# First ffn products beside the mixer's last norm, square sums one step later, running sums stored ahead of loads

## The chip, the core and the metric

One core of a Trainium2 chip runs the whole program in one launch. The time is the device time of an execution in microseconds (us); each kernel is run several times and the median counts. Shares and timelines come from one execution that the hardware profiler recorded.

## What is computed

Two transformer blocks over 512 tokens of width 1024, all in float32. The first block scales and shifts its input by a vector `c`, runs a mixer (a state-space scan beside attention), adds and normalizes, and runs an ffn with a squared relu. The second has a windowed attention with a gated unit and 32 routed experts. The change touches the first block alone:

```
h = x * (1.0 + sc1) + sh1
y = hybrid_mixer(h, ...)
x = layer_norm(ALPHA * x + (1.0 + g1) * y, ln1_g, ln1_b)
h = x * (1.0 + sc2) + sh2
ff = square(relu(h @ w_ff_in)) @ w_ff_out
x = layer_norm(ALPHA * x + (1.0 + g2) * ff, ln2_g, ln2_b)

# the end of hybrid_mixer
y_ssm = rms_norm(y * silu(z), ssm_norm_w)
y_att = rms_norm(attention, attn_norm_w)
y = concatenate([y_ssm, y_att]) @ w_out
```

## The kernel before

The program is a row of stages: prepare, streams, mixer, ffn, second, and router with experts. Each stage writes one queue of instructions per engine by hand (TensorE or PE, VectorE or DVE, ScalarE or ACT, GpSimd or POOL, SyncE or SP), and semaphores order them. A stage is a `Block`: at its end all engines meet in a barrier. Behind it stands a second, empty block (`run_stage`, L2867) in which SP clears every semaphore that the stage made, one instruction each, and then all meet again. Only router and experts share one block.

**Weights** go through a ring of four slots (`Weights`, L94). SP loads them in the order of a plan; `upto(sp, stop)` sends the loads up to an entry of the plan, and each load waits until PE has finished with what its slot held. In the plan stand, among others, `z 0`, `z 1` (the streams' last columns), eight `qkv` (one per pair of heads), four `out`, and `up` and `down` of the ffn. A load of 2 MB waits on its own slot alone, but SP's queue is in order, so what stands behind a waiting load waits too.

**Streams** (L348) makes the columns of the scan and of z with 20 groups of matmuls. DVE writes running sums into `sum_rows`; SP stores them to DRAM (L393, L394), behind all its loads of the stage. The mixer reads them back in a broadcast (L923, L928).

**Mixer** (L878): a loop of nine steps. In step j PE projects q, k, v of pair j, scans a chunk and attends for pair j-1; in the ninth step no pair is new, and PE makes the first half products of the out projection instead (`OutProjection`, L681). A tile is 128 tokens; a half product is 8 matmuls of 128x512, one half of the output columns of a tile over the scan's rows (`ssm`) or the attention's (`att`). For the rms norm ACT squares blocks of rows, POOL adds them up (`add_squares`), PE sums over partitions (`square_sums`, L787), and DVE makes the mean (`mean_square`, L823). The bank of these sums is one that a later half product needs, so PE waits for DVE there. In `rest` (L791) PE runs the attention's products for tiles 0 to 3; DVE adds and norms each tile (L839 to L870); PE turns it (`turn_x`, L800), and ACT copies it with scale and shift into `hT` (`columns`, L754; half of the last tile on DVE, L874).

**Ffn** (L1364): each of four groups of 1024 hidden columns has an up and a down product, and each such product is made from seven products of half-size blocks (`SevenProducts`, L1317) in the order P1, P2, P3, P7, P6, P5, P4. P1 and P2 take `hT` of tiles 0 and 1 as it is; the others take sums of `hT`'s quarters that DVE makes (`s_sums`), or weights that DVE has changed in the ring (`t_first`, `t_second`). In an up product one of the seven is 16 matmuls of 128x256 in four blocks (the profile counts each float32 matmul twice, as two passes). P6 goes into P1's banks, so ACT has to copy P1 out first (L1439), and it reads what `t_second` wrote; `t_second` stands on DVE's queue behind the joins that read that copy. At the stage's start POOL clears a tile of zeros, and ACT issues 16 stores of it, 512 KB each, to DRAM (L1435); they stand ahead of the copy of P1 on ACT's queue.

Of the kernel before, what the change touches and what calls it, by code (L numbers as in the profile page):

```python
# [347 lines left out]
def stage_streams(nc, A, G):  # L348

    with ExitStack() as ctx:
# [329 lines left out]
class OutProjection:  # L681
# [84 lines left out]
    def half(self, pe, t, h, k0, bank, depth, done):  # L766
        G = self.G
        for k in depth:
            if t == 0 and h == 0:
                pe.wait_ge(self.w_ok, k0 + k + 1)  # L770
            m = self.nc.tensor.matmul(G.ps[:, bank, :], G.mixT[:, k0 + k, t * P:(t + 1) * P],  # L771
                                      G.W.view(("out", (k0 + k) // 4))[:, k % 4, h * HALF:(h + 1) * HALF],
                                      start=(k == 0), stop=(k == KB - 1))
        if h == 1:
            m.then_inc(done, 1)
# [4 lines left out]
    def att(self, pe, t):  # L780
        for h in range(2):
            self.half(pe, t, h, KB, self.ATT[t][h], range(KB), self.y_done)
# [7 lines left out]

    def rest(self, pe):  # L791

        nc, G = self.nc, self.G

        def turn_x(t):
            pe.wait_ge(self.ln.ready, t + 1)
            if t:
                pe.wait_ge(self.h_ok, KB * t)
            for k in range(KB):
                m = nc.tensor.transpose(G.ps[:, self.TURN[k // 4], (k % 4) * P:(k % 4 + 1) * P], G.X[:, t, k * P:(k + 1) * P],  # L800
                                        G.ident[:])
            m.then_inc(self.turned, 1)
        pe.wait_ge(self.a_done, T)
        nc.tensor.nop().then_inc(G.W.used, 2)
        pe.wait_ge(self.ssm_read, 2)
        self.att(pe, 0)
        pe.wait_ge(self.ssm_read, 3)
        self.att(pe, 1)
        pe.wait_ge(self.ss_read, 2)
        turn_x(0)  # L810
        pe.wait_ge(self.ssm_read, 4)
        self.att(pe, 2)
        turn_x(1)
# [64 lines left out]
def stage_mixer(nc, A, G):  # L878
# [6 lines left out]
    with ExitStack() as ctx:  # L885
# [26 lines left out]
        block = ctx.enter_context(nc.Block())  # L912
# [129 lines left out]
        def _(pe):  # L1042
# [95 lines left out]
            for j in range(PAIRS + 1):  # L1138
# [62 lines left out]
        def _(dve):  # L1201
# [162 lines left out]
def stage_ffn(nc, A, G):  # L1364

    with ExitStack() as ctx:
# [16 lines left out]
        block = ctx.enter_context(nc.Block())  # L1384
# [75 lines left out]
        def _(pe):  # L1460
# [34 lines left out]

            def seven_products(f):
                for name in seven.ORDER:
                    operands_ready(f, name)
                    x, y = x_operand(f, seven.X_OF[name]), y_operand(f, seven.Y_OF[name])
                    for j in range(2):  # L1500
                        bank_ready(f, name, j)
                        out = bank(f, name, j)
                        if f % 2:
                            for k in range(4):
                                m = nc.tensor.matmul(out, x[:, k, j * P:(j + 1) * P], y[:, k, :],  # L1505
                                                     start=(k == 0), stop=(k == 3))
                        else:
                            for b in range(2):
                                at = (2 * j + b) * P
                                for k in range(4):  # L1510
                                    m = nc.tensor.matmul(out[:, b, :], y[:, k, at:at + P], x[:, k, :],  # L1511
                                                         start=(k == 0), stop=(k == 3))
                        m.then_inc(seven.done, 1)
# [12 lines left out]
            def last_down():  # L1526
# [24 lines left out]
        def _(dve):  # L1551
# [81 lines left out]
            def add(n):  # L1633
# [3 lines left out]
                nc.vector.tensor_tensor(y, y, ps[:, 4 + n % 4, :], ALU.add).then_inc(dn_read, 1)  # L1637
            s_sums(0, G.hT)
# [1227 lines left out]

def run_stage(nc, A, G, stage, last=False):  # L2867
# [17 lines left out]
def build(nc, A):  # L2885

    with ExitStack() as ctx:
# [4 lines left out]
        with ExitStack() as first:  # L2892
            G.W = Weights(nc, first, A)
            with ExitStack() as gates:
                G.gate = sbc(gates, "gates", [P, 2, D])
                mixed = ExitStack()
                G.mixT = sbc(mixed, "mixT", [P, 2 * KB, S])
                with ExitStack() as m:
                    G.xbcT = sbc(m, "xbcT", [P, XB, S])
                    G.w_dtf = sbc(m, "w_dtf", [P, KB, 32])  # L2900
                    G.head_rows = sbc(m, "head_rows", [P, 48])
                    G.d_col = sbc(m, "d_col", [P, KB])
                    G.dt = sbc(m, "dt", [P, T, 16])
                    G.av = sbc(m, "rates", [P, T, 32])
                    G.acs = sbc(m, "acs", [P, 64])
                    G.decays = sbc(m, "decays", [P, 128])
                    run_stage(nc, A, G, stage_prepare)
                    run_stage(nc, A, G, stage_streams)
                    G.X = ctx.enter_context(nc.sbuf_tensor("X", [P, T, D], F32, side="right"))
# [58 lines left out]
```

## Time and profile before

| | us |
|---|---|
| median of 3 runs | 2341.12 (2339.7 to 2341.65) |
| the profiled execution, its own time | 2340.7 |
| its span, first to last instruction | 2338.9 |
| streams, from PE's first matmul to the mixer's | 37.6 to 196.5 |
| mixer, to the ffn's first matmul | 196.5 to 600.0 |
| ffn, to the second block's first matmul | 600.0 to 1010.6 |

In a timeline a row is one instruction or several alike in a run: start, length from the first's start to the last's end, engine, line, operation, result and operands, count. In brackets stands how long the engine did nothing before, and who ended it.
### The profile page before, as it was taken

To read this page: it belongs to the slowest core of one execution; us is meant where nothing else is said; L and a number is where in the kernel's file an instruction comes from. 1 tells how busy PE (TensorE), PEld (TensorE's weight loads), DVE (VectorE), ACT (ScalarE), POOL (GpSimd) and SP (SyncE) were. 2 spreads that over 40 slices of the span, in tenths; PEclk is the share of its full clock that TensorE was granted. 3 is DMA by queue.
4 is the path that set the end of the run, shared out by engine and by line. 5 is a ranking of instruction groups with operands and counts; after the bars stand their busy time and mean duration, and the time that the engine had idled before them with its cause. 6 is when DMAs were issued, how large, how long until landed. Compare 5 with 4: busy or idle time off the path is not lost. (4 is left out here: it accounts for less than half of the span.)

```text
span 2338.9 us, 27117 instructions
## 1 busy us (share of the span) xinstructions
PE 2243.1 (96%) x9635; PEld 1068.9 (46%) x9636; DVE 869.9 (37%) x1582; ACT 646.1 (28%) x850; POOL 335.7 (14%) x289
## 2 busy tenths in 40 slices
PE   6998999999799999989898999999999999999997
PEld 2444665644657567535545333333333333333332
DVE  1882666633535365533534122111112111111126
ACT  1211223221010000002300543434343443444430
POOL 4461114440000000001200011010001000010112
PEclk8999999999899999999895999999999999999999
DMA  8463323302623121141007969999999999999997
GB/s 327 189 210 88 82 54 108 135 18 72 234 78 136 75 72 72 55 163 39 1 27 312 377 270 393 421 423 405 424 423 411 422 409 423 422 408 423 422 414 300
DMA packets 139445, 569.43 MB, mean 243 GB/s; under 512 B 12311, under 2 KB 47308, under 8 KB 88172
## 3 DMA queue, kind: packets, MB, share of 16 engines
q1 hardware_dynamic: 123584, 527.89, 57.0%
q0 software_dynamic: 6272, 20.62, 2.2%
q10 hardware_dynamic: 9516, 19.99, 2.2%
q8 instruction: 41, 0.67, 0.1%
q14 instruction: 32, 0.26, 0.0%
HBM read 544.53 MB, written 23.92 MB: 243 GB/s over the span
## 5 line engine op out<-in xcount | busy, mean ns | idle before, releaser
L2656 PE MATMUL banks<-expert_ring,slot_token_gate 128*64 128x512 f32 x2880 | 636.7, 594 | 5.4 <-DMA expert_ring<-in_w_up_dram 3.1
L2656 PEld LDWEIGHTS banks<-expert_ring,slot_token_gate 128*64 128x64 f32 x2880 | 202.3, 137 | 400.2 <-issue 387.0
L2592 ACT COPY expert_ring<-expert_ring 128x2048 f32 x176 | 324.5, 1896 | 75.6 <-DMA expert_ring<-in_w_gate_dram 64.2
L2656 PE MATMUL banks<-expert_ring,slot_xT_gate 128*64 128x512 f32 x1440 | 329.8, 600 | 1.7 <-issue 1.0
L2656 PEld LDWEIGHTS banks<-expert_ring,slot_xT_gate 128*64 128x64 f32 x1440 | 100.6, 138 | 189.3 <-issue 181.9
L2769 DVE TENSOR_SCALAR col_onehot<-banks,slot_gates 128x512 f32<-128x512 f32 x45 | 33.8, 750 | 402.8 <-PE banks L2656 402.7
L521 PE MATMUL banks<-hT,weight_ring 128*128 128x512 f32 x320 | 142.6, 605 | 3.6 <-DMA weight_ring<-in_w_in_dram 2.7
L2754 DVE TENSOR_TENSOR slot_token_gate<-banks,expert_bias_T 128x512 f32<-128x512 f32 x45 | 31.1, 691 | 297.4 <-PE banks L2626 296.4
L2512 POOL COPY slot_ids<-slot_tokens 128x1 int32 (+1 forms) x45 | 8.2, 183 | 891.7 <-PE banks L2626 891.7
L1511 PE MATMUL banks<-hT,weight_ring 128*128 128x256 f32 x512 | 114.5, 384 | 6.6 <-PEq L2878 5.7
L1054 PE MATMUL banks<-hT,weight_ring 128*128 128x512 f32 x256 | 116.1, 604 | 0.0
L771 PE MATMUL banks<-weight_ring,mixT 128*128 128x512 f32 x256 | 112.1, 594 | 3.4 <-DVE rms L823 3.4
L2566 ACT COPY col_onehot<-banks 128x512 f32<-128x512 f32 x45 | 26.4, 586 | 306.8 <-PE banks L2656 306.8
L1511 PEld LDWEIGHTS banks<-hT,weight_ring 128*128 128x128 f32 x512 | 98.2, 192 | 22.9 <-issue 9.4
L521 PEld LDWEIGHTS banks<-hT,weight_ring 128*128 128x128 f32 x320 | 61.2, 193 | 82.4 <-issue 79.5
L1505 PE MATMUL banks<-weight_ring,hidden_T 128*128 128x512 f32 x192 | 84.1, 593 | 0.9 <-PE banks L1511 0.9
L1511 PE MATMUL banks<-token_half_sums,weight_ring 128*128 128x256 f32 x384 | 84.2, 379 | 0.0
L1511 PEld LDWEIGHTS banks<-token_half_sums,weight_ring 128*128 128x128 f32 x384 | 73.0, 190 | 9.9
L771 PEld LDWEIGHTS banks<-weight_ring,mixT 128*128 128x128 f32 x256 | 47.8, 190 | 60.4 <-issue 56.8
L2626 PEld LDWEIGHTS banks<-ident,col_onehot 128*128 128x128 f32 x360 | 37.7, 140 | 75.3 <-issue 66.5
L1054 PEld LDWEIGHTS banks<-hT,weight_ring 128*128 128x128 f32 x256 | 47.6, 193 | 53.0 <-issue 53.0
L2572 ACT COPY col_onehot<-banks 128x512 f32<-128x512 f32 x45 | 26.3, 584 | 165.0 <-PE banks L2656 165.0
(454 smaller groups left out, 2570.3 us busy)
## 6 DMA issues: line engine op xcount, KB each, us to landing
expert_ring<-in_w_gate_dram SPq DMA_DIRECT2D x128, 1024.0 KB, 14.8
expert_ring<-in_w_up_dram SPq DMA_DIRECT2D x128, 1024.0 KB, 13.2
expert_ring<-in_w_down_dram SPq DMA_DIRECT2D x128, 1024.0 KB, 11.8
weight_ring<-in_w_ada_dram SPq DMA_DIRECT2D x12, 2048.0 KB, 11.9
weight_ring<-in_w_in_dram SPq DMA_DIRECT2D x8, 2048.0 KB, 12.1
weight_ring<-in_w_ff_in_dram SPq DMA_DIRECT2D x8, 2048.0 KB, 11.0
weight_ring<-in_w_ff_out_dram SPq DMA_DIRECT2D x8, 2048.0 KB, 10.6
weight_ring<-in_w_in_dram SPq DMA_DIRECT2D x24, 512.0 KB, 5.9
```

The lines of the kernel that those rows point to most:

```text
L521: m = nc.tensor.matmul(ps[:, n % 4, :], w[:, k, b * P:(b + 1) * P], G.hT[:, k, :], start=(k == 0), stop=(k == KB - 1))
L771: m = self.nc.tensor.matmul(G.ps[:, bank, :], G.mixT[:, k0 + k, t * P:(t + 1) * P], G.W.view(("out", (k0 + k) // 4))[:, k % 4, h * HALF:(h ...
L1054: x = nc.tensor.matmul(out, w[:, k, :], G.hT[:, k, :], start=(k == 0), stop=(k == KB - 1))
L1505: m = nc.tensor.matmul(out, x[:, k, j * P:(j + 1) * P], y[:, k, :], start=(k == 0), stop=(k == 3))
L1511: m = nc.tensor.matmul(out[:, b, :], y[:, k, at:at + P], x[:, k, :], start=(k == 0), stop=(k == 3))
L2566: nc.scalar.copy(side_by_side(gate_tok), paired(ps[:, B_G, :])).then_inc(q["g_copied"], 1)
L2572: nc.scalar.copy(side_by_side(up_tok), paired(ps[:, B_U, :])).then_inc(q["u_copied"], 1)
L2592: nc.scalar.copy(flat_ring[:, c * size:(c + 1) * size], flat_ring[:, bass.ds(source + c * size, size)])\
L2626: m = nc.tensor.transpose(ps[:, bank, j * P:(j + 1) * P], cols, G.ident[:])
L2656: x = nc.tensor.matmul(ps[h * CAP:(h + 1) * CAP, bank, :], lhs[:, k % 4, (k // 4) * CAP:(k // 4 + 1) * CAP], X.ring[:, m, k, h * HALF:(h + ...
L2754: nc.vector.tensor_tensor(up, turned_product(B_UT), cols, ALU.add).then_inc(q["u_biased"], 1)
L2769: nc.vector.tensor_scalar(to, ps[:, B_D, :], G.slot_gates[:, at], None, ALU.mult).then_inc(q["y_ok"], 1)
```

## The change

Three edits. The running sums are stored ahead of the load of z 1, and the last of the streams' loads (qkv 3) moves into the mixer's queue. In the mixer's ninth step PE makes the first square sums one step later, and DVE the mean square half a step sooner. And mixer and ffn share one block: the barrier and the clearing between them go, SP's and POOL's ffn parts wait for the last attention product, PE turns tile 2 inside the last attention product, then runs P1 and P2 of the first group with the turn of tile 3 in between.

```diff
--- before.py
+++ after.py
@@ stage_streams, SP @@
-            G.W.upto(sp, G.W.index[("qkv", 0)] + RING)
-
+            G.W.upto(sp, G.W.index[("z", 1)])
             sp.wait_ge(rows_ok, 2)
             sp.dma_start(G.sums_dram[0:16, :], rows[0:16, :]).then_inc(G.sums_out, 16)
             sp.dma_start(G.sums_dram[16:32, :], rows[32:48, :]).then_inc(G.sums_out, 16)
+            G.W.upto(sp, G.W.index[("qkv", 0)] + RING - 1)
@@ OutProjection.rest @@
         pe.wait_ge(self.y_read, 1)
-        self.att(pe, 3)
+        self.att(pe, 3, 0)
+        self.att(pe, 3, 1, range(0, KB // 2))
+        self.turn_x(pe, 2)
+        self.att(pe, 3, 1, range(KB // 2, KB))
         pe.wait_ge(self.y_done, T)
         nc.tensor.nop().then_inc(G.W.used, 2)
-        turn_x(2)
-        turn_x(3)
@@ stage_mixer, PE @@
                     pe.wait_ge(q["proj_read"], 3 * PAIRS)
                     out.ssm(pe, 0, 1)
-                    pe.wait_ge(q["y_read"], PAIRS)
-                    out.square_sums(pe, 0)
                 if old:
...
                 else:
+                    pe.wait_ge(q["y_read"], PAIRS)
+                    out.square_sums(pe, 0)
                     pe.wait_ge(q["state_ready"], PAIRS)
                     out.ssm(pe, 1, 0)
@@ stage_mixer, DVE @@
                 if new:
                     ssm_out(j)
+                else:
+                    out.mean_square(dve, 0)
                 if old:
                     turned(U + 4)
                     softmax(U + 6)
-                    if not new:
-                        out.mean_square(dve, 0)
                     turned(U + 6)
@@ stage_ffn, SP and POOL @@
+            sp.wait_ge(out.y_done, T)
             ln.load(sp)
...
+            pool.wait_ge(out.y_done, T)
             nc.gpsimd.memset(zeros[:], 0.0).then_inc(zeros_ok, 1)
@@ stage_ffn, PE @@
+            def first_products():
+
+                G.W.wait(pe, ("up", 0, 0))
+                pe.wait_ge(out.h_ok, 2 * KB)
+                pe.wait_ge(out.y_read, 3)
+                for j in range(2):
+                    for b in range(2):
+                        up_block(0, "P1", j, b)
+                up_block(0, "P2", 0, 0)
+                out.turn_x(pe, T - 1)
+                up_block(0, "P2", 0, 1)
+                for b in range(2):
+                    up_block(0, "P2", 1, b)
+                pe.wait_ge(out.y_read, T)
+                pe.wait_ge(out.h_ok, T * KB)
+
             def seven_products(f):
-                for name in seven.ORDER:
+                for name in seven.ORDER[2:] if f == 0 else seven.ORDER:
...
+            first_products()
             for f in range(LAST):
                 seven_products(f)
@@ stage_ffn, DVE @@
+            dve.wait_ge(out.h_ok, T * KB)
             s_sums(0, G.hT)
@@ the stages @@
+def stage_mixer_to_ffn(nc, A, G):
+
+    with ExitStack() as ctx:
+        G.block = ctx.enter_context(nc.Block())
+        stage_mixer(nc, A, G)
+        G.mixer_tiles.close()
+        stage_ffn(nc, A, G)
+
...
-                    run_stage(nc, A, G, stage_mixer)
-                mixed.close()
-                run_stage(nc, A, G, stage_ffn)
...
+                run_stage(nc, A, G, stage_mixer_to_ffn)
```

On SP's queue, at the end of streams (`X`, `key_bias`: what the mixer reads of the sums; `weight_ring` 128x8x128: a third of a `qkv` load; `ISA`: the clears). Before:

```order
L141 DMA weight_ring<-in_w_in_dram 128x8x512
L141 DMA weight_ring<-in_w_in_dram 128x8x128 x12
L393 DMA running_sums<-sum_rows 16x512
L394 DMA running_sums<-sum_rows 16x512
L351 UNCONDITIONAL_BRANCH
```

Now:

```order
L392 DMA running_sums<-sum_rows 16x512
L393 DMA running_sums<-sum_rows 16x512
L141 DMA weight_ring<-in_w_in_dram 128x8x512
L141 DMA weight_ring<-in_w_in_dram 128x8x128 x9
L351 UNCONDITIONAL_BRANCH
```

The stores stand ahead of z 1 and three of the four pairs; the fourth pair's three loads went to the next stage.

On PE's queue, in the mixer's ninth step (`ident,probs`: turns of two units; `kT,qT` and `causal_bf`: logits; `mixT`: half products; `ones,xbcT`: the square sums). Before:

```order
L771 MATMUL banks<-weight_ring,mixT 128x512 x8
L787 MATMUL banks<-ones,xbcT 128x1 x4
L1090 MATMUL banks<-ident,probs 128x128 x4
L1076 MATMUL banks<-kT,qT 128x384 x2
L1079 MATMUL banks<-causal_bf,ident_bf 128x128 x2
L771 MATMUL banks<-weight_ring,mixT 128x512 x8
```

Now:

```order
L771 MATMUL banks<-weight_ring,mixT 128x512 x8
L1096 MATMUL banks<-ident,probs 128x128 x4
L1082 MATMUL banks<-kT,qT 128x384 x2
L1085 MATMUL banks<-causal_bf,ident_bf 128x128 x2
L786 MATMUL banks<-ones,xbcT 128x1 x4
L771 MATMUL banks<-weight_ring,mixT 128x512 x8
```

The sums went behind two turns and a step's logits.

On PE's queue, at the mixer's end (`ident,X`: turns of a tile, 8 each; 128x256: blocks of the ffn's products). Before:

```order
L771 MATMUL banks<-weight_ring,mixT 128x512 x16
L800 MATMUL banks<-ident,X 128x128 x16
L885 UNCONDITIONAL_BRANCH
L1459 UNCONDITIONAL_BRANCH
L1511 MATMUL banks<-hT,weight_ring 128x256 x32
L1511 MATMUL banks<-token_half_sums,weight_ring 128x256 x16
```

Now:

```order
L771 MATMUL banks<-weight_ring,mixT 128x512 x12
L797 MATMUL banks<-ident,X 128x128 x8
L771 MATMUL banks<-weight_ring,mixT 128x512 x4
L1468 UNCONDITIONAL_BRANCH
L1509 MATMUL banks<-hT,weight_ring 128x256 x20
L797 MATMUL banks<-ident,X 128x128 x8
L1509 MATMUL banks<-hT,weight_ring 128x256 x12
L1509 MATMUL banks<-token_half_sums,weight_ring 128x256 x16
```

Tile 2 is turned four matmuls ahead of the attention's end, tile 3 behind 20 of the 32 matmuls of P1 and P2, and one branch is left of two with a barrier between. On ACT's queue the order is the same as before: the copies of all four tiles, the 16 stores of zeros, the two copies of P1.

## Rows read from the trace of the kernel before

**Rows 1.** The page: busy time of PE; DMA share in 40 slices
```profile
PE 2243.1 (96%) x9635; PEld 1068.9 (46%) x9636; DVE 869.9 (37%) x1582; ACT 646.1 (28%) x850; POOL 335.7 (14%) x289
...
DMA  8463323302623121141007969999999999999997
```

**Rows 2.** Timeline, streams' end (start us, us, engine, line, op, [idle before <-releaser])
```profile
189.53 0.60 ACT L456 ACTIVATE mixT<-banks 128x512 f32<-128x512 f32 x1 [6.71 <-PE banks L521]
...
193.25 0.42 SPq L394 DMA_DIRECT2D running_sums<-sum_rows  x1
```

**Rows 3.** Timeline of PE, start of the mixer, and a later projection
```profile
196.46 1.09 PE L1109 MATMUL banks<-ident,xbcT 128*128 128x128 f32 x4 [6.96 <-PEq L2878]
...
197.98 15.30 PE L1054 MATMUL banks<-hT,weight_ring 128*128 128x512 f32 x32
...
224.09 7.09 PE L1054 MATMUL banks<-hT,weight_ring 128*128 128x512 f32 x16
```

**Rows 4.** Windows (us, busy of PE, PEld, DVE, ACT, POOL, PEclk, DMA)
```profile
194.00:195.00 1.00, 0.00 (x0) 0.00 (x0) 0.00 (x0) 0.00 (x0) 0.00 (x0) 0.50 1.22 290
...
201.00:202.00 1.00, 1.00 (x4) 0.43 (x3) 0.00 (x0) 0.00 (x0) 0.00 (x0) 1.00 0.64 144
...
488.00:489.00 1.00, 0.00 (x0) 0.00 (x0) 0.80 (x3) 0.98 (x3) 0.00 (x0) 1.00 0.00 0
```

**Rows 5.** Timeline of PE, the mixer's last step
```profile
474.47 1.02 PE L787 MATMUL banks<-ones,xbcT 128*128 128x1 f32 x8 [1.14 <-POOL xbcT L732]
...
489.32 7.13 PE L771 MATMUL banks<-weight_ring,mixT 128*128 128x512 f32 x16 [3.42 <-DVE rms L823]
```

**Rows 6.** Timelines of POOL and DVE, the same step
```profile
468.83 5.49 POOL L732 TENSOR_TENSOR xbcT<-xbcT 128x512 f32<-128x512 f32 x4 [1.26 <-ACT xbcT L741]
...
479.48 0.80 DVE L1223 TENSOR_SCALAR probs<-probs,att_stats 128x384 f32<-128x384 f32 x1
```

**Rows 7.** Timeline of PE, last norm and first ffn products
```profile
585.18 1.06 PE L800 MATMUL banks<-ident,X 128*128 128x128 f32 x8 [0.30 <-PE banks L771]
...
600.03 15.79 PE L1511 MATMUL banks<-hT,weight_ring 128*128 128x256 f32 x64 [5.70 <-PEq L2878]
615.66 7.07 PE L1511 MATMUL banks<-token_half_sums,weight_ring 128*128 128x256 f32 x32
...
629.47 13.98 PE L1511 MATMUL banks<-token_half_sums,weight_ring 128*128 128x256 f32 x64
```

**Rows 8.** Timeline of ACT, the same stretch
```profile
589.36 2.89 ACT L754 ACTIVATE hT<-banks,mod_cols 128x128 f32<-128x128 f32 x8
594.37 1.51 ACT L754 ACTIVATE hT<-banks,mod_cols 128x128 f32<-128x128 f32 x4 [2.12 <-PE banks L800]
600.97 19.42 ACTq L1435 DMA_DIRECT2D expert_rows<-zeros  x16
620.44 1.07 ACT L1439 COPY hidden_T<-banks 128x512 f32<-128x512 f32 x2 [24.56 <-issue]
```

**Rows 9.** Timeline of DVE, the same stretch
```profile
603.69 1.22 DVE L1344 TENSOR_TENSOR hT<-hT 128x1024 f32<-128x1024 f32 x1
...
623.59 2.28 DVE L1359 TENSOR_TENSOR weight_ring<-weight_ring 128x2048 f32<-128x2048 f32 x1
```

**Rows 10.** The line that issues the zero stores (duration ns, first and last start)
```profile
L1435 ACTq DMA_DIRECT2D expert_rows<-zeros x16: 396/1272/1902, 601.0 to 619.1; - x16
```

**Rows 11.** Timeline, ffn to the second block, and that to the router
```profile
1007.98 0.69 DVE L1671 COPY hT<-banks 128x512 f32<-128x512 f32 x1 [1.91 <-PE banks L1522]
...
1010.55 0.34 SPq L1725 DMA_DIRECT2D sink_row<-in_sinks_dram  x1
...
1235.22 0.13 DVE L2120 TENSOR_SCALAR neg_top<-top 128x1 f32<-128x1 f32 x1
...
1239.00 0.38 ACTq L2214 DMA_DIRECT2D hT<-in_b_gate_dram  x1
```

**Rows 12.** Timeline of PE, router to experts inside one merged block
```profile
1263.89 3.95 PE L2402 MATMUL banks<-place_onehot,hT 32*128 32x32 f32 x32
```

More of the change, by code:

```diff
@@ L773, in half @@
                                       start=(k == 0), stop=(k == KB - 1))
-        if h == 1:
+        if h == 1 and KB - 1 in depth:
             m.then_inc(done, 1)
@@ L778, in ssm, with att @@
         self.half(pe, t, h, 0, self.SSM[t][h], depth, self.a_done)
-    def att(self, pe, t):
-        for h in range(2):
-            self.half(pe, t, h, KB, self.ATT[t][h], range(KB), self.y_done)
+    def att(self, pe, t, h, depth=range(KB)):
+        self.half(pe, t, h, KB, self.ATT[t][h], depth, self.y_done)
     def square_sums(self, pe, m):
@@ L789, in square_sums, with turn_x @@
         x.then_inc(self.ss_done, 1)
+    def turn_x(self, pe, t):
+        G = self.G
+        pe.wait_ge(self.ln.ready, t + 1)
+        if t:
+            pe.wait_ge(self.h_ok, KB * t)
+        for k in range(KB):
+            m = self.nc.tensor.transpose(G.ps[:, self.TURN[k // 4], (k % 4) * P:(k % 4 + 1) * P], G.X[:, t, k * P:(k + 1) * P],
+                                         G.ident[:])
+        m.then_inc(self.turned, 1)
     def rest(self, pe):
         nc, G = self.nc, self.G
[L795 to L802, printed above, removed]
         pe.wait_ge(self.a_done, T)
@@ L911, in stage_mixer @@
         out = OutProjection(nc, ctx, A, G)
-        block = ctx.enter_context(nc.Block())
+        G.out = out
+        block = G.block
         @block.sync
@@ L1383, in stage_ffn @@
         ln = Norm(nc, ctx, G, "ln2", A["ln2_g"][0:1, :], A["ln2_b"][0:1, :])
-        block = ctx.enter_context(nc.Block())
+        out = G.out
+        block = G.block
         def x_quarter(src):
@@ L1494, in bank_ready, with up_block @@
                     pe.wait_ge(seven.joined, 16 * g + 3 + j)
+            def up_block(f, name, j, b):
+                x, y = x_operand(f, seven.X_OF[name]), y_operand(f, seven.Y_OF[name])
+                at = (2 * j + b) * P
+                for k in range(4):
+                    m = nc.tensor.matmul(bank(f, name, j)[:, b, :], y[:, k, at:at + P], x[:, k, :],
+                                         start=(k == 0), stop=(k == 3))
+                if b:
+                    m.then_inc(seven.done, 1)
@@ new lines, in down_block @@
+            def down_block(f, name, j):
+                x, y = x_operand(f, seven.X_OF[name]), y_operand(f, seven.Y_OF[name])
+                for k in range(4):
+                    m = nc.tensor.matmul(bank(f, name, j), x[:, k, j * P:(j + 1) * P], y[:, k, :],
+                                         start=(k == 0), stop=(k == 3))
+                m.then_inc(seven.done, 1)
+            def first_products():
[12 more added lines that the diff above has]
+                pe.wait_ge(out.h_ok, T * KB)
@@ L1496, in seven_products @@
             def seven_products(f):
-                for name in seven.ORDER:
+                for name in seven.ORDER[2:] if f == 0 else seven.ORDER:
                     operands_ready(f, name)
-                    x, y = x_operand(f, seven.X_OF[name]), y_operand(f, seven.Y_OF[name])
                     for j in range(2):
                         bank_ready(f, name, j)
-                        out = bank(f, name, j)
                         if f % 2:
-                            for k in range(4):
-                                m = nc.tensor.matmul(out, x[:, k, j * P:(j + 1) * P], y[:, k, :],
-                                                     start=(k == 0), stop=(k == 3))
+                            down_block(f, name, j)
@@ L1507, in seven_products @@
                         else:
                             for b in range(2):
[L1509 to L1513, printed above, removed]
+                                up_block(f, name, j, b)
                 pe.wait_ge(seven.done, 14 * (f + 1))
@@ L2895, in build @@
                 G.gate = sbc(gates, "gates", [P, 2, D])
[L2896 to L2909, printed above, removed]
-                    run_stage(nc, A, G, stage_mixer)
-                mixed.close()
-                run_stage(nc, A, G, stage_ffn)
+                G.mixer_tiles = m = ExitStack()
+                G.mixT = sbc(m, "mixT", [P, 2 * KB, S])
+                G.xbcT = sbc(m, "xbcT", [P, XB, S])
+                G.w_dtf = sbc(m, "w_dtf", [P, KB, 32])
+                G.head_rows = sbc(m, "head_rows", [P, 48])
+                G.d_col = sbc(m, "d_col", [P, KB])
+                G.dt = sbc(m, "dt", [P, T, 16])
+                G.av = sbc(m, "rates", [P, T, 32])
+                G.acs = sbc(m, "acs", [P, 64])
+                G.decays = sbc(m, "decays", [P, 128])
+                run_stage(nc, A, G, stage_prepare)
+                run_stage(nc, A, G, stage_streams)
+                G.X = ctx.enter_context(nc.sbuf_tensor("X", [P, T, D], F32, side="right"))
+                run_stage(nc, A, G, stage_mixer_to_ffn)
             G.w_router = ctx.enter_context(nc.sbuf_tensor("w_router", [P, KB, EXPERTS], F32, side="right"))
```

13 lines of the change are left out of this document (8 added, 5 removed).

## The prediction, made before the changed kernel was run

> **What bounds the kernel now.** I read the page first. TensorE is busy for 96% of the span, and the DMA slices are mostly under half up to slice 21 and full from slice 25 on [rows 1]: up to the router the kernel is bound by PE's chain with its gaps, in the experts by the stream of weights. The stages run one behind the other, so what a gap loses ahead of the router comes off the end, unless something behind was waiting for other reasons; the diff touches nothing there. So the question is which of PE's gaps close. I went along PE's timeline and looked at each idle time of over 1 us, then at the engine named as its releaser.
>
> Three places matter. At the streams' end PE stands still for 6.96 us [rows 3]. ACT's last work ends at 190.13, but SP issues its second store of the running sums as late as 193.25 to 193.67 [rows 2]: SP holds the barrier. The granted clock falls to 0.50 (1.2 GHz) in this gap and is back at 1.00 (2.4 GHz) by 201 [rows 4]. In the mixer's last step PE waits 1.14 us for POOL's sum of squares and 3.42 us for DVE's mean square [rows 5]. At the mixer's end PE turns tile 2 at 585.18, then tile 3 waits, then comes the barrier; the ffn starts at 600.03 [rows 7], at half clock.
>
> **The change part by part.** I keep the times of before as the ruler, each part against its own place.
>
> *Sums stored ahead of loads (A).* The two stores move ahead of the z 1 load, far ahead of PE's end; the three loads of pair 3, which wait for z 1's products, move into the mixer behind its first two small loads. They aren't needed before pair 3. SP has nothing left to do at the end, so the last is ACT at 190.13 [rows 2]. What the barrier takes is bounded by the others: 196.46 less 193.67 = 2.8 us here with 28 semaphores to clear, and 1010.55 less 1008.67 = 1.9 us with 24 [rows 11]. I take 2.5: PE starts at 192.6, 3.9 us sooner. Its gap is then 3.1 us, and over a gap of 3.42 us the clock stayed at 1.00 [rows 4, 5]. So the slow start should go too: 1.1 us by 15.30 against twice 7.09 [rows 3], at most 2.3 (half of 196.46 to 201). I take 1.8, which the same slow start costs in the ffn (15.63 us from start to start for 64 matmuls against 13.81) [rows 7]. A gives 5.7 us.
>
> *Square sums a step later (B).* PE, free at 473.33 (474.47 less the wait), now turns two units and makes the next logits first, ten instructions; I estimate 1.5 us for them, and POOL is done at 474.32 [rows 6]. DVE takes the mean square behind the softmax that ends at 480.28 [rows 6] and no longer behind the next one; PE asks for it at 489.32 - 4.6 = 484.7. DVE doesn't wait for it, as the sums are made by 476. Both waits go: 1.14 + 3.42 = 4.6 us. Nothing else is late: the softmax that now follows has the 7.13 us of the next half product to hide in [rows 5].
>
> *The ffn in the mixer's block (C).* Tile 2 is turned inside the last attention product, which ends 0.9 us later (eight transposes, 1.06 us [rows 7]), at 585.8; with 0.3 us of wait P1 starts at 586.1. It needs tiles 0 and 1 alone. P1 and one of P2's four blocks are 40 of 64 matmuls of 0.216 us [rows 7], 8.6 us: 594.7. Tile 3 is normed by then (ACT's copy of tile 2 ends at 592.25 + 0.9 [rows 8]) and is turned without a wait, until 595.6. Copies of it take 1.5 us [rows 8], the four sums on DVE 4.9 us (600.03 to 604.91 [rows 9]): the third product can start at 602.1, while PE ends P2 at 600.8. 1.3 us lost. Third and fourth take 13.8 us [rows 7]: PE is at the fifth (P6) at 615.9, 13.6 us sooner than 629.47.
>
> But P6 needs the bank of P1 and weights that DVE makes after it read P1's copy, and ACT copies P1 only behind its 16 stores of zeros. These took 600.97 to 620.39, then the copies from 620.44 [rows 8], and DVE's weights were ready at 625.87 [rows 9], 5.4 us behind the copies' start. Before, that was 3.6 us ahead of PE, so it cost nothing; now that cover is gone. In the new order the stores still stand behind ACT's last copies, which end at 597.2. With the same 19.5 us the P1 copies start at 616.7, the weights are there at 622.1, and P6 starts at 622.2: 7.2 us sooner, with a gap of 6.3 us ahead of it. Over such a gap the clock fell [rows 3, 4], so the slow start of 1.8 us that the ffn's beginning had is only moved to P6. The loss of the old start lies within 629.47; the new one comes behind 622.2. So C gives 7.2 - 1.8 = 5.4 us.
>
> Is 19.5 us right? The 16 issues have a median of 1272 ns, a shortest of 396 and a longest of 1902 [rows 10]; 512 KB each in 1272 ns is 412 GB/s, so I hold the train for bound by the transfer and not by ACT. The 4 MB of down weights are asked for at 585.8, as before at 585.0, and by the rate of the train take some 10 us: they are through when the stores begin. Only the two rows of gain and shift stand beside the stores, as before. The Trainium skill (DMA: Bandwidth & Descriptors, "Issuing engines are not separate DMA queues") says that SP's and ACT's transfers share the same 16 DMA engines and interleave; by it, loads still under way would stretch the train, and the sum would turn into the third rival's, while the rows give the one above.
>
> The branch at the seam costs nothing visible: router and experts lie in one block like this, and PE's 32 matmuls across that seam take 3.95 us without a gap [rows 12].
>
> *The longer clear (D).* The mixer's 54 semaphores are no longer cleared at 596 to 600 but with the ffn's 24 at the next barrier. Barriers took 1.88 us with 24, 3.65 with 55 [rows 11], 4.15 with 54 (595.88 to 600.03 [rows 7, 8]): 0.057 to 0.076 us each, so 3.1 to 4.1 us more. I take 3.4. It falls on the chain; nothing covers it.
>
> Sum: 5.7 + 4.6 + 5.4 - 3.4 = 12.3 us. The profiled execution's own time is 2340.7 us (span 2338.9), 0.4 us under the median of the three: **2328.4 us**.
>
> **The rivals.** *The train does not bind.* If ACT's issues go at the shortest one's 396 ns [rows 10], they end at 603.5, the weights are ready by 612, and P6 starts at 615.9 with no gap before it. C gives 13.6: 20.5 us in all, 2320.2 us. Against it: the median.
>
> *The streams' end isn't SP's.* If the barrier waits for something else, or for the stores' landing as well, A gives nothing: 2334.1 us. For it: a barrier of 2.8 us with 28 semaphores is longer than the 0.06 us each would make it (2.1); against it: SP is the only engine with work after 190.13.
>
> *The train is slowed by the loads it now meets.* Place: ACT's queue from 597. If ACT's stores get half of the DMA engines all along, an issue takes 2.43 us, the train ends at 636.1, P6 starts at 641.6, 12.1 us later than before. 5.7 + 4.6 - 12.1 - 1.8 - 3.4 = -7.0: 2347.7 us, slower. It decides from a train of 31.8 us on, 1.99 us an issue; the longest single issue was 1902 ns [rows 10]. It needs 8 MB of loads beside the stores, and some 1 MB is left by then.
>
> **How the numbers follow.** Forecast 0.74, streams 0.13, train that doesn't bind 0.06, slow train 0.03; 0.04 is left for a new wait of a few us in the mixer's first step, whose small loads I only moved. The bounds of the unknown costs: A 4.6 to 6.6, train 1.5 us either way, D 3.1 to 4.1: 2325 to 2332 for the forecast alone. Taking in the streams' rival gives **2323.5 to 2334.5**. A measurement of this kernel can tell 0.2%, 4.7 us. Faster by more than that are the forecast, the first two rivals and part of the rest: 0.91. Slower 0.03, the same 0.06.
>
> **What would show it.** In the new profile: PE's gap ahead of the mixer is near 3 us and the clock stays at 1.00; no wait of PE for POOL's squares or DVE's mean square; PE's matmuls of P1 run on from the attention's; a gap of 1 to 2 us ahead of the third product; a gap of about 6 us ahead of P6, released by DVE, with ACT's stores of zeros ending just under 6 us before its end; a barrier of about 5.3 us between ffn and second block. I am wrong if P6 has no gap, if the gap is over 10 us, if the first gap stays near 7, or if the experts' stage changes its length by more than 2 us.

## The result, and the profile after

The kernel after takes 2320.67 us in the median of five (2314.18 to 2323.31), the kernel before beside it 2339.7 (2335.32 to 2341.65): a ratio of 0.9913, interval 0.9892 to 0.9934. That is 19.0 us less where 12.3 were forecast, below the range's lower end of 2323.5. The profiled execution of after took 2315.37 us (span 2313.2), 25.7 us less of span than that of before.

Where it came from, in the two profiled executions (shift: how much sooner the same instruction starts than in before):

| place | before | after | shift | gained here | on record |
|---|---|---|---|---|---|
| ACT's last work in streams | 189.53 | 188.33 | 1.2 | 1.2 | not part of the change (below) |
| first half product of the mixer | 213.20 | 208.33 | 4.87 | A 3.7 | 5.7 |
| half product behind the mean square | 489.32 | 479.54 | 9.78 | B 4.9 | 4.6 |
| P6, the ffn's fifth product | 629.47 | 606.47 | 23.0 | C 13.2 | 5.4 |
| second block's first projection | 1010.60 | 991.17 | 19.4 | D -3.6 | -3.4 |
| router's first count | 1241.08 | 1215.40 | 25.7 | 6.3 | 0 |

The streams' last matmul ends at 186.5 to 189.5 us in the thirteen profiles of this document, whichever order the stores have (189.50 in before, 186.58 in e7, which has the same streams), so the 1.2 us are one execution's and not the change's.

The timelines of ACT and PE at the mixer's start answer to [rows 2, 3], the windows to [rows 4]:

```profile
188.33 0.60 ACT L456 ACTIVATE mixT<-banks 128x512 f32<-128x512 f32 x1 [6.71 <-PE banks L521]
```

```profile
191.51 0.63 PE L1115 MATMUL banks<-ident,xbcT 128*128 128x128 f32 x4 [3.22 <-PEq L2922]
...
192.30 15.60 PE L1060 MATMUL banks<-hT,weight_ring 128*128 128x512 f32 x32
208.33 1.09 PE L1135 MATMUL banks<-X 128*64 128x128 f32 x16 [0.43 <-DVE X L1260]
```

```profile
193.00:194.00 1.00, 1.00 (x2) 0.44 (x2) 0.00 (x0) 1.00 (x1) 0.00 (x0) 0.50 0.57 158
...
197.00:198.00 1.00, 1.00 (x4) 0.51 (x3) 0.53 (x1) 0.53 (x1) 0.00 (x0) 1.00 0.97 243
```

The barrier runs from ACT's end at 188.93 to 191.51, 2.6 us, and PE's gap is 3.2 instead of 7.0 us. But the clock falls to 0.50 behind this gap too, so the 32 projections keep a slow start (15.60 us, 15.30 before), and there is a new wait of 0.43.

In the mixer's last step both waits of [rows 5] are gone:

```profile
469.80 1.00 PE L786 MATMUL banks<-ones,xbcT 128*128 128x1 f32 x8
...
479.54 7.09 PE L771 MATMUL banks<-weight_ring,mixT 128*128 128x512 f32 x16
```

At the seam, PE's timeline against [rows 7]:

```profile
571.46 1.04 PE L797 MATMUL banks<-ident,X 128*128 128x128 f32 x8
...
576.23 8.87 PE L1509 MATMUL banks<-hT,weight_ring 128*128 128x256 f32 x40 [0.30 <-PE banks L771]
584.94 1.04 PE L797 MATMUL banks<-ident,X 128*128 128x128 f32 x8
585.81 5.35 PE L1509 MATMUL banks<-hT,weight_ring 128*128 128x256 f32 x24
592.58 7.14 PE L1509 MATMUL banks<-token_half_sums,weight_ring 128*128 128x256 f32 x32 [1.42 <-DVE hT L1350]
599.56 7.07 PE L1509 MATMUL banks<-hT,weight_ring 128*128 128x256 f32 x32
606.47 13.98 PE L1509 MATMUL banks<-token_half_sums,weight_ring 128*128 128x256 f32 x64
```

Up to the third product all is as forecast: the 40 matmuls take 8.87 us (8.6 on record), the wait ahead of the third is 1.42 (1.3). The gap of 6.3 us ahead of P6 isn't there. ACT's timeline, and ACT's issues of zeros with their landing (shortest, median, longest), show why, against [rows 8, 10]:

```profile
586.01 0.46 ACT L754 ACTIVATE hT<-banks,mod_cols 128x128 f32<-128x128 f32 x1 [2.72 <-PE banks L797]
586.02 0.40 ACTq L1444 DMA_DIRECT2D expert_rows<-zeros  x1
...
587.45 11.20 ACTq L1444 DMA_DIRECT2D expert_rows<-zeros  x13
598.69 1.07 ACT L1448 COPY hidden_T<-banks 128x512 f32<-128x512 f32 x2 [11.17 <-issue]
```

```profile
L1444 ACTq DMA_DIRECT2D expert_rows<-zeros x16: 396/549/1330, 586.0 to 597.3; - x16
...
DMA to landing us min/median/max: 7.0/12.9/15.1
```

The 16 issues take 12.6 us instead of 19.4, a median of 549 ns instead of 1272, and a store lands 12.9 us behind its issue (median) instead of 7.4. What stands beside the stores has changed, too: SP asked for the two rows of gain and shift at 600.0, just ahead of the stores, and asks for them at 577.0 now, right behind the down weights. SP's timeline of before, then of after:

```profile
600.00 0.34 SPq L647 DMA_DIRECT2D ln_gb<-in_ln_g_dram  x1
600.39 0.45 SPq L648 DMA_DIRECT2D ln_gb<-in_ln_b_dram  x1
```

```profile
576.05 0.92 SPq L141 DMA_DIRECT2D weight_ring<-in_w_ff_out_dram  x2
577.01 0.50 SPq L647 DMA_DIRECT2D ln_gb<-in_ln_g_dram  x1
577.56 0.65 SPq L648 DMA_DIRECT2D ln_gb<-in_ln_b_dram  x1
```

ACT copies P1 at 598.69, DVE's weights are made 601.84 to 604.12, and PE comes to P6 at 606.47 without a gap. At the ffn's end the barrier takes from 985.81, the end of DVE's last copy, to 991.17, 5.4 us for 78 clears [rows 11]:

```profile
991.17 9.31 PE L1851 MATMUL banks<-hT,weight_ring 128*64 128x512 f32 x34 [6.08 <-PEq L2922]
```

The last 6.3 us lie in the second block, which the diff doesn't touch. PE waits 2.37 us there for POOL's probabilities in both kernels; what differs is the clock behind the wait. Timeline and windows of before, then of after:

```profile
1121.88 1.53 PE L1871 MATMUL banks<-ident,probs 128*128 128x128 f32 x8 [2.37 <-POOL probs L1753]
1123.34 3.78 PE L1858 MATMUL banks<-k2T,q2T 64*128 64x256 f32 x8
```

```profile
1125.00:1130.00 5.00, 5.00 (x22) 3.24 (x22) 4.06 (x13) 0.87 (x2) 0.00 (x0) 0.50 0.00 0
```

```profile
1101.30 1.09 PE L1906 MATMUL banks<-ident,probs 128*128 128x128 f32 x8 [2.37 <-POOL probs L1788]
1102.33 1.99 PE L1893 MATMUL banks<-k2T,q2T 64*128 64x256 f32 x8
```

```profile
1104.00:1109.00 5.00, 5.00 (x27) 2.67 (x26) 4.05 (x13) 3.51 (x5) 0.00 (x0) 1.00 0.00 0
```

### The profile page after: what moved, and what is told of

Same layout as the page of the kernel before. It is cut to its first block and busy times, and to the rows that moved or that the text cites. A ratio compares the mean times of both kernels' runs of the same rounds, so it can differ in the third digit from the quotient of the medians.

```text
span 2313.2 us, 27097 instructions
## 1 busy us (share of the span) xinstructions
PE 2232.4 (97%) x9635; PEld 1062.1 (46%) x9636; DVE 871.8 (38%) x1582; ACT 646.2 (28%) x850; POOL 336.0 (15%) x289
```

## The experiments

The question was why the train of zeros is short now, what each part is worth by itself, and whether the second block's 6.3 us belong to the change. Ratios are against the kernel before, run beside each.

**The parts apart (e1, e2).** e1, against the kernel after (of its three edits the third is undone; one hunk of it is shown):

```diff
...
-                run_stage(nc, A, G, stage_mixer_to_ffn)
+                    run_stage(nc, A, G, stage_mixer)
+                mixed.close()
+                run_stage(nc, A, G, stage_ffn)
...
```

> The kernel before with the first two parts alone (sums stored ahead of loads, square sums a step later), mixer and ffn in blocks of their own. By the trace after, the first part is worth 3.7 us (a shift of 4.9 us behind the mixer's first half product, of which 1.2 us stood already ahead of the barrier) and the second 4.9: 8.6 us, a time of about 2331 us. By the terms on record 5.7 + 4.6 = 10.3 us: 2329.4 us. In the profile: a gap of about 3.2 us ahead of the mixer, no wait for POOL's squares or DVE's mean square, and ACT's stores of zeros still a train of 19.5 us.

Measured: 2327.02 us (2322.07 to 2331.01), ratio 0.9946 [0.9931, 0.9961], 12.6 us less by the ratio (9.1 at least). The profile has the gap of 3.27 us at the mixer's start, no wait in the last step, and the train 19.0 us long (591.05 to 610.01). More was gained than the profiles' 8.6; e7 takes that up.

e2, against the kernel after (the first two edits undone, the third kept):

```diff
-            G.W.upto(sp, G.W.index[("z", 1)])
+            G.W.upto(sp, G.W.index[("qkv", 0)] + RING)
             sp.wait_ge(rows_ok, 2)
...
+                    pe.wait_ge(q["y_read"], PAIRS)
+                    out.square_sums(pe, 0)
                 if old:
...
                 else:
-                    pe.wait_ge(q["y_read"], PAIRS)
-                    out.square_sums(pe, 0)
...
```

> The kernel after without its first two parts: mixer and ffn in one block alone. Theory of the short train (read from the trace after): ACT's 16 stores of zeros take some 12.6 us from the first issue to the end of the last, ACT copies P1 before PE asks for its bank, PE starts P6 without a gap: 13.2 - 3.4 = 9.8 us, about 2330 us. Theory on record (train of 19.5 us, gap of 6.3 us and a slow start of 1.8 us): 5.4 - 3.4 = 2.0 us, about 2338 us.

Measured: 2332.2 us (2326.15 to 2337.29), ratio 0.9966 [0.9953, 0.9978]: 5.1 to 11.0 us less, with 9.8 in it and 2.0 not. The train takes 12.8 us (597.04 to 609.84), and PE starts P6 at 617.48, 30.2 us behind P1, as in after, without a gap.

**The train held back (e3),** against the kernel after:

```diff
             act.wait_ge(zeros_ok, 1)
+            act.wait_ge(ln.gain_in, 32)
+            G.W.wait(act, ("down", 0, 1))
```

> The kernel after, in which ACT starts its stores of zeros only when the second down load and both rows of gain and shift have landed (some 6.6 us later, near 592.6 us). Theory that loads in front make the issues short: with none in front only the first four issues take about 0.5 us and the others 1.27, the train is 19.5 us again, ends near 612, P1's copies 613, DVE's weights near 617.7, and PE waits some 11 us ahead of P6 and then starts it at half clock: 11 + 1.8 = 13 us slower than the kernel after, about 2333 us. Rival, that the train is short because it is issued in the mixer's block or beside an ACT and PE at work: 12.6 us again, it ends near 605.3, PE waits about 4 us ahead of P6: 4 to 6 us slower than after, 2325 to 2327 us.

Measured: 2328.9 us (2324.1 to 2333.05), ratio 0.996 [0.9946, 0.9973]. ACT's and PE's timelines:

```profile
591.14 18.27 ACTq L1446 DMA_DIRECT2D expert_rows<-zeros  x16
609.45 1.07 ACT L1450 COPY hidden_T<-banks 128x512 f32<-128x512 f32 x2 [22.30 <-issue]
```

```profile
614.93 15.95 PE L1511 MATMUL banks<-token_half_sums,weight_ring 128*128 128x256 f32 x64 [8.68 <-DVE weight_ring L1365]
```

With nothing in front, the train is 18.3 us again, inside the same block and beside the same work. PE waits 8.7 us (11 were expected; the loads had landed at 591.1 instead of 592.6, 1.5 us sooner) and starts P6 at half clock: 64 matmuls in 15.95 us instead of 13.98. The time, 2328.9, is some 9 us above the kernel after (2319.9, the median of its eleven times below); 13 were expected. The forecast had a kernel with such a train and gave it 2328.4 us. That the two agree is in part luck: the wait ahead of P6 is 2.4 us longer than the 6.3 forecast, and the first two edits gain more in the times than the 10.3 us forecast (e1).

**Loads put in front of the train of the kernel before (e4),** against before:

```diff
-        G.W.upto(sp, G.W.index[("up", 0, 0)] + RING)
+        G.W.upto(sp, G.W.index[("up", 0, 0)] + 2)
```

> The kernel before, in which SP issues the two down loads (4 MB) at the ffn's start, just behind the rows of gain and shift and just as ACT begins its zeros, instead of at the mixer's end. Theory that loads in front make the issues short: eight or more issues of 0.4 to 0.6 us, then about 1.1 us each, a train of 12 to 14 us with landings that grow to 12 us and more. Rival that the issues are bound by their own transfer: 19.5 us. Rival on record that loads beside it share the engines and stretch it: 25 to 32 us. PE comes to P6 27 to 29 us behind the first issue in all cases, so the time stays within 0.2% of before, but for the last rival with a train of 32 us, which would cost up to 10 us.

Measured: 2338.73 us (2334.89 to 2343.36), ratio 1.0001 [0.9991, 1.001]. ACT's issues:

```profile
L1435 ACTq DMA_DIRECT2D expert_rows<-zeros x16: 396/797/3502, 602.9 to 622.0; - x16
...
DMA to landing us min/median/max: 8.3/19.0/23.0
```

Each theory had a part of it. Loads in front do make the first issues short: nine of 0.4 to 0.9 us pass (three in before). But then come six of 1.6 to 2.4 and one of 3.5, 22.5 us in all, as the loads stretch the stores. PE comes to P6 29.5 us behind the first issue and does not wait, so the time is the same. The first eight stores land 2.3 to 2.7 us apart, the rest 1.2 to 1.3. The Trainium skill (DMA: Bandwidth & Descriptors, "Issuing engines are not separate DMA queues") says that transfers issued by different engines share the 16 DMA engines and interleave; the landings, at half pace while the loads move, agree.

**The two rows behind the train (e9),** against the kernel after:

```diff
             sp.wait_ge(out.y_done, T)
+            sp.wait_ge(G.y_zeroed, 16 * (-(-(LIST - EXPERTS) * CAP // P)))
             ln.load(sp)
             G.W.upto(sp, G.W.index[("q2",)] + RING)
-            sp.wait_ge(G.y_zeroed, 16 * (-(-(LIST - EXPERTS) * CAP // P)))
```

> The kernel after, in which SP loads the ffn's two rows of gain and shift (1 MB) behind the zeros instead of ahead of them, so that only the two down loads are still moving when ACT issues its first store at 585.5 to 586 us. Theory that issues are quick until the first store of the train itself moves: the loads are through by about 588 instead of 592.6, the first store lands near 589.5 instead of 593, four to six issues are quick instead of nine or ten, the rest take 1.0 to 1.3 us, and the train is 15 to 16 us instead of 12.6; PE then waits up to 1 us ahead of P6. Rival, that a train is short whenever it is issued in one block with the mixer: 12.6 us and nine or ten quick issues again.

One time, 2321.1 us. ACT's issues and PE's timeline:

```profile
L1444 ACTq DMA_DIRECT2D expert_rows<-zeros x16: 396/1232/1544, 584.2 to 601.5; - x16
...
DMA to landing us min/median/max: 4.1/6.4/6.6
```

```profile
608.24 15.77 PE L1509 MATMUL banks<-token_half_sums,weight_ring 128*128 128x256 f32 x64 [3.42 <-DVE weight_ring L1365]
```

A train of 18.5 us with two quick issues, and PE waits 3.4 us and starts P6 at half clock. The effect is stronger than the 15 to 16 us expected, and it speaks against the rival that a train in one block with the mixer is always short: the 1 MB of rows in front makes the whole difference, as the down weights are still landing here as well (until 587.0). In after the down weights land until 588.8 and the rows until 592.6, and ACT's first ten issues pass meanwhile.

**The squares alone, and after again (e7, e6).** e7 is the kernel before with the square sums' edit of the change alone (the hunks of PE and DVE in stage_mixer); e6 has no edit.

> The kernel before with the square sums moved alone. On record 4.6 us: 2333.6 us. Theory that the two waits also make the clock fall in many executions (in two of the three profiles that still have both waits it fell at one or both, and the stretch to the last attention product was 2.9 and 5.5 us longer than in the profiled execution of before): 4.9 us and some 2 to 3 more in the median, about 2331 us, and a narrower spread than before's 2334.9 to 2345.3.

> The kernel after, unchanged, for its spread and for a second profile. Theory that the second block's 6.2 us are the clock of one execution of the kernel before and no part of the change: 224.2 to 224.3 us from the second block's first projection to the router's first count, as in the kernel after and in all four experiments so far, unless the clock falls in its attention as it did at 1122 us in the kernel before. Median 2319 to 2322 us. Rival, that the shorter second block belongs to the change: nothing new here, but then the kernel before with loads moved would not have shown 224.3 us.

e7: 2329.89 us (2327.48 to 2330.05), ratio 0.9959 [0.9947, 0.9972], 9.6 us less by the ratio, 6.5 at least. That is more than the two waits' 4.6 us. In the two other profiles that still have both waits the clock falls behind them, which it didn't in before [rows 4, 5]: behind both in e2, behind the second in e4. From the first square sums to the end of the attention's products e4 takes 2.9 us longer than before and e2 4.6 (5.5 with the turn of tile 2, which lies inside this stretch only in e2). So falls of the clock are the likely rest of e7's gain; how often before has them in its other executions was not measured. PE's timeline of e2, with 16 matmuls in 10.12 us instead of 7.13 [rows 5]:

```profile
471.03 1.02 PE L786 MATMUL banks<-ones,xbcT 128*128 128x1 f32 x8 [1.14 <-POOL xbcT L732]
...
487.52 10.12 PE L771 MATMUL banks<-weight_ring,mixT 128*128 128x512 f32 x16 [3.42 <-DVE rms L828]
```

e6: 2317.17 us (2312.26 to 2324.91), ratio 0.9915 [0.9897, 0.9933]; its second block takes 224.2 us (990.53 to 1214.72). With the five times above, after's eleven lie in two groups, five at 2312.3 to 2315.4 and six at 2319.9 to 2324.9 (median 2319.9). Eight profiles (after, e1 to e4, e6, e7, e9) have a second block of 224.2 to 224.3 us, three of them with mixer and ffn in blocks of their own as in before (e1, e4, e7); of the kernels so far only before's own has 230.5. So the 6.3 us are no part of the change. The upper group of after's times goes with the clock: the mean granted clock of the five lower executions is 0.982 or 0.983, of the six upper ones 0.978 to 0.980. That is 0.003 of 2313 us less clock, an estimate of 7 us lost, and the groups' medians lie 8 us apart. In which stage the clock fell is not known, as no profile of an upper one was taken.

**The clears off the chain (e5, e11).** To see whether a barrier costs what it clears, the kernel after was changed to clear a stage's semaphores on SP within the next stage, and the block that cleared them between two stages goes (the second block keeps its own; the hunks in `run_stage` are shown in part):

```diff
+    def clear(sp):
+        for s in old[1]:
+            sp.sem_clear(s)
...
             G.W.upto(sp, G.W.index[("z", 1)])
+            G.clear(sp)
...
+                if j == 1:
+                    G.clear(sp)
...
             G.W.upto(sp, len(G.W.plan))
+            G.clear(sp)
```

> The kernel after, in which SP clears the semaphores of a stage inside the next stage, while it has nothing to issue, instead of in a block of their own between the two (streams: prepare's 16; mixer: the streams' 28; second block: the 78 of mixer and ffn; the second block's own 55 stay at its barrier). Theory that the length of a barrier is its clears, some 0.063 us each: the barrier ahead of the mixer falls from 2.6 us to under 1 and PE's gap there from 3.2 to about 1.5, over which the clock stays at 1.00 (worth 1.8 + 2.2 us); the one ahead of the second block falls from 5.3 to under 1 (worth 4.5); the first is hidden behind weight loads. 8 to 9 us faster than after, about 2312 us. Rival, that a barrier takes its time whatever is cleared in it, or that the loads of the second block, which land until 989.8 us, hold PE there instead: 2 to 4 us faster, about 2317 us.

Measured: 2313.41 us (2308.72 to 2320.34), ratio 0.9897 [0.988, 0.9914]; again, as e11, 2311.99 (2306.98 to 2315.85), 0.9877 [0.9859, 0.9895].

> The kernel of e5, unchanged, beside e10 and for its spread. Median within 3 us of 2313.4 us; 6 to 8 us under the kernel after (2319.9 us, the median of its 11 runs).

PE's timeline of e5:

```profile
188.79 0.63 PE L1118 MATMUL banks<-ident,xbcT 128*128 128x128 f32 x4 [0.94 <-PEq L351]
...
189.58 13.90 PE L1063 MATMUL banks<-hT,weight_ring 128*128 128x512 f32 x32
205.62 1.09 PE L1138 MATMUL banks<-X 128*64 128x128 f32 x16 [2.13 <-DVE X L1263]
...
983.43 2.83 PE L1855 MATMUL banks<-hT,weight_ring 128*64 128x512 f32 x6 [1.05 <-PEq L2908]
```

The gap ahead of the second block falls from 6.08 to 1.05 us, so 5.0 us of it were the 78 clears. At the mixer's start the gap is 0.94, the clock stays at 1.00 and the projections take 13.90 instead of 15.60; but PE then waits 2.13 us for a chain of ACT, POOL and DVE that didn't come sooner. This has the lowest median here, 2313.3 us in its ten times, 6.5 under after's eleven (3.8 under e6, which ran beside e5), where 8 to 9 were expected. A part of what is missing shows in the profiles: in all four with the short barriers (e5, e8, e10, e11) the second block took 230.5 to 233.1 us, its clock falling behind the 2.37 us wait as in before. Why there, and not in the eight others with long barriers, is open.

**The fourth pair's loads elsewhere (e8, e10).** POOL starts its first product of the mixer 7.1 us behind the mixer's start in before, 10.9 in after and e5. Both runs are e5 with the loads that the change put there moved on; e8 left them to the second step's other loads, e10 put them between that step's rows (the diff is e10's; e8 has its last hunk alone):

```diff
+                if j == 1:
+                    G.W.upto(sp, G.W.index[("qkv", 0)] + RING + 1)
                 if j:
                     sp.wait_ge(q["logits_read"], UNITS * j)
...
-                G.W.upto(sp, G.W.index[("qkv", 0)] + RING + j + 1)
+                if j:
+                    G.W.upto(sp, G.W.index[("qkv", 0)] + RING + j + 1)
```

> The kernel of e5, in which SP issues the loads of the fourth pair of heads (3 x 512 KB) only with the second step's loads instead of right behind the first step's rows of sums. In the kernels after and e5 these three loads land beside the rows and POOL starts its first product 10.9 us behind the mixer's start instead of 7.1 as in the kernel before, which PE pays with 0.43 us (after) and 2.13 us (e5) of waiting for DVE ahead of the first half product. Theory that these loads hold up POOL's start: it starts about 7 us behind the mixer's start again, PE's wait of 2.13 us is gone, 2 us faster than e5, about 2311 us. Rival, that POOL's start is late for another reason (what it ran before, the shorter barrier): 10.9 us again, the wait stays, 2313 us.

> The kernel of e5, in which SP issues the loads of the fourth and fifth pair of heads between the second step's two rows of sums: away from the first step's rows, where after and e5 have the fourth, and ahead of the third step's rows, behind which e8 let them collide. Theory that in e8 PE's new waits of 4.9 and 1.7 us in the second step came from the third step's row of sums landing behind nine loads: these waits are gone, the wait ahead of the first half product stays near 0.5 us instead of e5's 2.1, 1 to 2 us faster than e5, about 2312 us. Rival, that the loads collide with whatever comes there: a new wait of over 2 us somewhere in the first two steps, 2314 us or more.

e8: 2324.01 us (2315.5 to 2327.31), some 10 us more than e5 where 2 less were expected. POOL starts 9.3 us behind, not 7.1. Nine loads now stand in one row ahead of the third step's sums, which SP asks for at 256.7 instead of 246.6, and PE has a new wait:

```profile
268.79 0.69 PE L1100 MATMUL banks<-ident,probs 128*128 128x128 f32 x2 [4.88 <-DVE probs L1233]
```

e10: 2313.75 us (2309.38 to 2315.57), that wait gone and the first one 1.38 us, but POOL still 10.1 us behind: no gain over e5 that can be told. So these loads are not the main cause of POOL's late start. It stays open; no run here touches one thing that the traces show: POOL's queue has two `MODIFY_POOL_CONFIG` within 0.1 us of the mixer's start in every profile, and then nothing until the product, without a wait that the profile can name.

## Why the prediction was wrong

It named the right places and the right sign, and missed the size mainly by one step: by the times, the joint block gives 7.9 us (e2) where C less D was 2.0, and the other two edits 12.6 (e1) where A and B were 10.3.

**The step that failed is the train of zeros in C:** "With the same 19.5 us the P1 copies start at 616.7", and behind it "they are through when the stores begin. Only the two rows of gain and shift stand beside the stores, as before." The train took 12.6 us, so the gap of 6.3 us ahead of P6 and the slow start of 1.8 fell away, 8.1 us; C is 13.2 instead of 5.4. The start of the train was right to 1.4 us (586.02, which is 595.8 on before's ruler; 597.2 on record). The loads were not. With the ffn's SP part in the mixer's block, the two rows are asked for at 577.0, right behind the down weights and ahead of the stores, and land until 592.6. And the down weights are not through: the second lands at 588.8, 12.8 us behind the first one's request and 2.8 us behind the first store's issue, where the forecast had 10 us by the train's rate (12.9 in before, 585.0 to 597.9). Taking the rows away from there (e9) or waiting for all the loads (e3) brings the train back to 18.5 and 18.3 us, and PE's gap to 3.4 and 8.7 us: shown.

The mistake in reading was to take an issue of 1272 ns for the time that its 512 KB must take, because the quotient looked like a transfer rate. In before the two did go together, as the stores landed mostly 1.23 to 1.30 us apart. In after they land as far apart, but ten issues, 5 MB, pass in 5.7 us, and the first of their stores lands behind the last of them. The Trainium skill (Perfetto Trace Analysis, "DMA Instruction — HWDGE (DVE, Sync)") says that the length shown for such an instruction covers the making of its descriptors and not the movement of the data; these ten agree.

When issues pass quickly can be told from the thirteen profiles as far as this: with at most 2 MB of loads still to land at the first issue (before, e1, e3, e7, e9) two or three pass in under 0.7 us and the train takes 16.3 to 19.4 us; with 3 MB (after, e2, e5, e6, e8, e10, e11) eight to ten do and it takes 12.6 to 13.4; with 5 MB (e4) eight of the first nine do, but the later ones make it 22.5. Why the loads do this is open. That an issue turns slow when its own queue's stores begin to move does not fit: in before the fourth issue takes 1.63 us and ends at 604.13, and the first packet of ACT's queue moves at 604.44.

**The rival that came true by its result,** "the train does not bind" (C 13.6, 2320.2 us), had a chance of 0.06 because the median spoke against it. Its mechanism, 396 ns an issue all along, did not come, so that its time came out is in part luck; it was enough that the train ended before about 601 us, 5.4 us ahead of PE at P6.

**A, 3.7 instead of 5.7.** The barrier (2.6 for 2.5) and the gap (3.2 for 3.1) came as forecast. "So the slow start should go too" did not: that the clock stayed at 1.00 over a gap of 3.42 us in one execution of before was no rule, as it fell over the same gap in e2 and e4, and over the 3.2 us here in all five profiles with it (the 32 projections take 14.65 to 15.60 us there, 13.90 in e5, where the clock stays). A wait of 0.43 us is the new wait in the first step for which 0.04 was left.

**B, 4.9 for 4.6** in the two profiled executions; both waits went and nothing else came late. e7 shows that it is worth more (9.6 us, 6.5 at least) in the times, most likely because the clock falls behind those waits in other executions, as in e2 and e4. The prediction put this at nothing; the slow start of 1.8 us that A did not save goes the other way.

**D, 3.6 for 3.4.** The barrier took 5.4 us with 78 clears, and e5 shows that 5.0 us of the gap are clears.

**Slow train and streams' end,** the other rivals: e4 shows the first one's mechanism, stores landing at half pace beside loads, but nine issues are through by then; the second is excluded by the gap of 3.2 us.

## What to carry to other kernels

The length of a DMA issue is not given by its bytes: issues of the same 512 KB took 0.4 to 3.5 us here, by what was in flight. Before a train of issues is moved, look at what will be in flight when it starts and ask what the issues cost at the shortest and at the longest seen, not at the median. If an engine has compute behind such a train, where its loads stand decides when that compute runs; here 1 MB ahead of the stores or behind them was 6 us of ACT's time. Clears of semaphores cost 0.06 to 0.08 us each on the chain at the two barriers where they were taken off (5.0 us for 78, 2.3 for 28), and can be done a stage later while the queue is idle.

## What the runs showed that was not expected

The same wait of PE leaves the clock at 1.00 in one execution and takes it to 0.50 in another: 2.37 us in the second block (kept in eight profiles, fallen in five), 3.42 us in the mixer (kept in one, fallen in two). Even the 1.14 us ahead of the square sums did so (kept in two, fallen in one, e2). The stretches with such falls are 3 to 9 us longer here. So a small wait can be worth more in the median than its own length, and one profile's stage can differ from another's by 6 us with the same code.
